# A two-layer RWKV-7 / mLSTM trunk on one core: the triangular inversion on all four quarters of TensorE, and layer norms scaled in one VectorE step

## What is computed

```python
def _layer_norm(x, g, b):
    mu = x.mean(-1); var = mean(square(x - mu))
    return (x - mu) * rsqrt(var + 1e-5) * g + b

def _layer(x, st, w):
    x = _layer_norm(ALPHA * x + 0.5 * _swiglu(x, ffn1...), ln1_g, ln1_b)      # norm 0
    p = x @ w_in
    ya = _rwkv7(p[..., :RWKV_COLS], ...)      # S = S*w + sa (kk*a) + v k per token, 8 heads of 64
    yb = _mlstm(p[..., RWKV_COLS:], ...)      # 4 heads of 128
    x = _layer_norm(ALPHA * x + concat(ya, yb) @ w_out, ln2_g, ln2_b)         # norm 1
    x = _layer_norm(ALPHA * x + 0.5 * _swiglu(x, ffn2...), ln3_g, ln3_b)      # norm 2
```

## Time and profile before

| | us |
|---|---|
| median of 3 runs | 1639.91 (1639.57 to 1642.65) |
| the profiled execution, its own time | 1636.58 |
| its span | 1634.5 |
| PE busy / weight loads busy | 1549.8 (95%) / 1486.7 (91%) |
| DVE / ACT / POOL busy | 865.3 (53%) / 665.4 (41%) / 416.1 (25%) |

### The profile page before, as it was taken

How to read it: one execution, slowest core, us unless ns; L and a number is a source line. 1 busy time by engine, 2 the same in 40 slices (tenths; PEclk the granted TensorE clock), 3 DMA queues, 4 the chain that set the end, 5 groups by cost and what they waited for, 6 DMA issues and landing times.

```text
span 1634.5 us, 34807 instructions
## 1 busy us (share of the span) xinstructions
PE 1549.8 (95%) x13868; PEld 1486.7 (91%) x13868; DVE 865.3 (53%) x1347; ACT 665.4 (41%) x1071; POOL 416.1 (25%) x427
## 2 busy tenths in 40 slices
PE   7999999999998899999899999999999998999994
PEld 7999998998977799999799999989978787999993
DVE  4444436686356764444464444366944577444334
ACT  4333235656432443333343333357563245333323
POOL 6222552013121432221052221020132324222011
PEclk9999999999997899999999999999999899999997
DMA  7455552442122555544354545434330443544420
GB/s 205 144 151 150 160 152 71 124 112 75 28 62 78 149 147 148 154 143 153 103 147 144 151 143 165 118 96 111 96 76 3 115 119 108 164 143 152 148 97 32
DMA packets 307200, 197.75 MB, mean 121 GB/s; under 512 B 7516, under 2 KB 282320, under 8 KB 307096
## 3 DMA queue, kind: packets, MB, share of 16 engines
q1 hardware_dynamic: 303512, 189.64, 39.9%
q0 software_dynamic: 3584, 6.62, 1.6%
HBM read 187.46 MB, written 8.78 MB: 120 GB/s over the span
## 4 chain that ended last, share of the span: by engine, by line
PE 89%; DVE 5%; ACT 3%; POOL 1%; DVEq 1%; issue 1%; DMA 0%; ACTq 0%; POOLq 0%
PE bank L1905 25%; PE bank L1907 24%; PE bank L1906 24%; PE bank L674 1%; PE bank L690 1%; PE bank L585 1%; PE bank L686 1%; PE bank L561 1%; PE bank L1976 1%; POOL xl L2349 1%; PE bank L423 1%; DVE x L2250 1%; PE bank L1978 1%; PE bank L433 1%; DVE z L2248 1%
## 5 line engine op out<-in xcount | busy, mean ns | idle before, releaser
L1905 PE MATMUL bank<-xh,whi 128*128 128x320 f32 x2016 | 632.8, 314 | 31.6 <-POOL xl L2379 24.7
L2217 DVE TENSOR_TENSOR wlo<-raw,whi 128x1024 fp32r<-128x1024 f32 x340 | 428.2, 1262 | 401.2 <-ACT whi L2101 400.5
L1906 PE MATMUL bank<-xl,whi 128*128 128x320 f32 x2016 | 628.5, 312 | 0.0
L1907 PE MATMUL bank<-xh,wlo 128*128 128x320 f32 x2016 | 628.2, 312 | 0.0
L2101 ACT ACTIVATE whi<-raw 128x1024 fp32r<-128x1024 f32 x340 | 359.2, 1060 | 573.9 <-PE bank L1907 569.4
L1905 PEld LDWEIGHTS bank<-xh,whi 128*128 128x128 f32 x2016 | 383.6, 190 | 38.4 <-issue 32.6
L1906 PEld LDWEIGHTS bank<-xl,whi 128*128 128x128 f32 x2016 | 383.8, 190 | 0.5
L1907 PEld LDWEIGHTS bank<-xh,wlo 128*128 128x128 f32 x2016 | 383.4, 190 | 0.0
L2359 POOL TENSOR_TENSOR hl<-scratch,hh 128x320 f32 x88 | 146.1, 1661 | 435.9 <-DVE scratch L2270 435.9
L1905 PE MATMUL bank<-hh,whi 128*128 (+1 forms) x704 | 218.4, 310 | 0.7 <-ACT vec L2137 0.7
L1907 PE MATMUL bank<-hh,wlo 128*128 (+1 forms) x704 | 217.2, 309 | 0.0
(11 more groups left out here) (363 smaller groups left out, 1568.0 us busy)
## 6 DMA issues: line engine op xcount, KB each, us to landing
raw<-in_ffn_wg SPq DMA_DIRECT2D x88, 512.0 KB, 3.8
raw<-in_ffn_wu SPq DMA_DIRECT2D x88, 512.0 KB, 3.8
raw<-in_ffn_wd SPq DMA_DIRECT2D x88, 512.0 KB, 3.6
raw<-in_w_in SPq DMA_DIRECT2D x60, 512.0 KB, 3.8
raw<-in_w_out SPq DMA_DIRECT2D x16, 512.0 KB, 5.4
raw<-in_state_C SPq DMA_DIRECT2D x8, 512.0 KB, 6.5
out_s_C<-raw SPq DMA_DIRECT2D x8, 512.0 KB, 3.5
ring<-in_state_wkv POOLq DMA_DIRECT2D x2, 1024.0 KB, 8.5
```

Source lines behind the costliest of these rows:

```text
L1905: pe.matmul(out, w_hi, hi, start=start, stop=False)
L1906: pe.matmul(out, w_hi, lo, start=False, stop=False)
L1907: return pe.matmul(out, w_lo, hi, start=False, stop=stop)
L2217: dve.tensor_tensor(wlo[:, slot, :], raw[:, slot, :], whi[:, slot, :].bitcast(F32), ALU.subtract).then_inc(lo_ready.sem, 1)
```

## The change

**Norms.** The sums are made with `means` (1/1024 in place of 1), so they are the means. ACT squares the mean from the bank, DVE needs two steps for the variance, copies the mean, and subtracts it from six tiles in pairs ahead of the root. One DVE step (`scalar_tensor_tensor`) multiplies a tile by gain and root; ACT adds the bias into `xh`; DVE makes `xl` = (z + bias) - xh itself (`low`), one tile later; POOL has no part in it. ACT writes the full `x` of all eight tiles after the eight `xh`. `first_chunks` does the two passes with `xh` as soon as `xh` of a k is there, and that with `xl` one k later. The last norm makes only `x`, on ACT, and the turns at the end wait for it.

**Inversion.** `xx` keeps, for half q, xi in rows q and xti in the other rows, so that both are in one area of 128 partitions; `copy_growth` makes two copies of 256 columns, from bank 2 + q each (banks 0 and 1 too in the first level), where one of 512 was made. `grow` issues its 16 matmuls in turns over all four quarters of the array; `product`, `samples_u` and the recurrence's products use the crossed quarters. `grow` of step n now waits for the copy of step n - 1. `first_growth` makes 16 matmuls for xi and xti, where 8 and a DVE mask were. POOL's `memory_term` is cut into two halves of 64 columns.

```diff
         def first_growth(pe, L, c):
             pe.wait_ge(t1_ready.sem, t1_ready.by(L, c + 1))
@@
             for j in range(NJ):
-                for part in PART:
-                    last = pe.matmul(bank[2 + c % 2][part, j * CH:(j + 1) * CH], xti[part, c, j, :],
-                                     ident[part, part], start=True, stop=True)
+                for q, part in enumerate(PART):
+                    pe.matmul(bank[growth_bank(c) + q][part, j * CH:(j + 1) * CH], t1[part, c, j, :], ident[part, part],
+                              start=True, stop=True)
+                for q, part in enumerate(PART):
+                    last = pe.matmul(bank[growth_bank(c) + q][PART[1 - q], j * CH:(j + 1) * CH], ident[part, part],
+                                     t1[part, c, j, :], start=True, stop=True)
@@ def grow(pe, L, n):
-            pe.wait_ge(x_copied.sem, x_copied.by(L, n - 1))
-            if lv < NLV[c] - 1:
-                for j in range(NJ):
-                    for part in PART:
-                        pe.matmul(bank[2 + n % 2][part, j * CH:(j + 1) * CH], xti[part, c, j, :], t1[part, c, j, :],
+            pe.wait_ge(x_copied.sem, x_copied.by(L, n))
+            for j in range(NJ):
+                if lv < NLV[c] - 1:
+                    for q in range(2):
+                        pe.matmul(bank[2 + q][PART[q], j * CH:(j + 1) * CH], xti(q, c, j), t1[PART[1 - q], c, j, :],
                                   start=True, stop=True)
-            for j in range(NJ):
-                for part in PART:
-                    last = pe.matmul(bank[2 + n % 2][part, (NJ + j) * CH:(NJ + j + 1) * CH], t1[part, c, j, :],
-                                     xti[part, c, j, :], start=True, stop=True)
+                for q in range(2):
+                    last = pe.matmul(bank[2 + q][PART[1 - q], j * CH:(j + 1) * CH], t1[PART[1 - q], c, j, :],
+                                     xti(q, c, j), start=True, stop=True)
@@ def copy_growth(act, L, n):
-            lo, hi = int(lv == NLV[c] - 1), 1 + int(lv > 0)
-            act.activation(xx[:, c, lo:hi, :, :].rearrange("p x j s -> p (x j s)"),
-                           bank[2 + n % 2][:, lo * NJ * CH:hi * NJ * CH], ACT.Copy).then_inc(x_copied.sem, 1)
+            for q in range(2):
+                rows = slice(0, P) if lv < NLV[c] - 1 else PART[1 - q]
+                last = act.activation(xx[rows, c, q, :, :].rearrange("p j s -> p (j s)"), 
+                                      bank[growth_bank(n) + q][rows, 0:NJ * CH], ACT.Copy)
+            last.then_inc(x_copied.sem, 1)
@@ def first_chunks(base, which, outs):  (PE)
-                    for k in range(KT):
-                        pe.wait_ge(x_ready.sem, x_ready.by(L, KT * (which - 1) + k + 1))
-                        for n in range(LOOK):
-                            last = three_passes(pe, outs[n], slot_of(L, base + n), k * P, xh[:, k, :], xl[:, k, :],
+                    for k in range(KT + 1):
+                        if k < KT:
+                            pe.wait_ge(xh_ready.sem, xh_ready.by(L, before + k + 1))
+                            for n in range(LOOK):
+                                slot = slot_of(L, base + n)
+                                for w in (whi, wlo):
+                                    pe.matmul(outs[n], w[:, slot, k * P:(k + 1) * P], xh[:, k, :],
+                                              start=(k == 0 and w is whi), stop=False)
+                        if k:
+                            pe.wait_ge(x_ready.sem, x_ready.by(L, before + k))
+                            for n in range(LOOK):
+                                last = pe.matmul(outs[n], whi[:, slot_of(L, base + n), (k - 1) * P:k * P],
+                                                 xl[:, k - 1, :], start=False, stop=(k == KT))
@@ def layer_norm(which):  (ACT)
+                    act.wait_ge(stats_ready.sem, stats_ready.by(L, which + 1))
+                    act.activation(rstd, LN_SUMS[which][0][:, 0:T], ACT.Square).then_inc(msq_ready.sem, 1)
@@
-                        act.activation(xh[:, o, :], z[:, o, :], ACT.Identity, scale=g, bias=b).then_inc(
-                            xh_ready.sem, 1)
+                        if not last_norm:
+                            act.activation(xh[:, o, :], z[:, o, :], ACT.Identity,
+                                           bias=vec[:, g0 + KT + o:g0 + KT + o + 1]).then_inc(xh_ready.sem, 1)
+                    for o in range(KT):
+                        act.activation(x[:, o, :], z[:, o, :], ACT.Identity,
+                                       bias=vec[:, g0 + KT + o:g0 + KT + o + 1]).then_inc(xf_ready.sem, 1)
@@ def layer_norm(which):  (DVE)
+                    dve.wait_ge(msq_ready.sem, msq_ready.by(L, which + 1))
+                    dve.scalar_tensor_tensor(out=var, in0=sums[1], scalar=eps, in1=rstd,
+                                             op0=ALU.add, op1=ALU.subtract)
+                    dve.drain()
+                    dve.tensor_scalar(var, var, eps, None, ALU.max).then_inc(var_ready.sem, 1)
+                    dve.tensor_copy(mean, sums[0])
...
+                    for o in range(0, KT - 2, 2):
+                        dve.tensor_tensor(z[:, o:o + 2, :], z[:, o:o + 2, :],
...
-                        dve.tensor_tensor(z[:, o, :], z[:, o, :], rstd, ALU.mult).then_inc(norm_ready.sem, 1)
-                        if o + 4 < KT:
-                            dve.tensor_tensor(z[:, o + 4, :], z[:, o + 4, :], mean, ALU.subtract)
+                        dve.scalar_tensor_tensor(out=z[:, o, :], in0=z[:, o, :], scalar=vec[:, g0 + o:g0 + o + 1],
+                                                 in1=rstd, op0=ALU.mult, op1=ALU.mult).then_inc(norm_ready.sem, 1)
+                        if o + 6 < KT:
+                            dve.tensor_tensor(z[:, o + 6, :], z[:, o + 6, :], mean, ALU.subtract)
                         dve.drain()
-                        dve.tensor_scalar(x[:, o, :], z[:, o, :], g, b, ALU.mult, ALU.add).then_inc(xf_ready.sem, 1)
+                        if o and not last_norm:
+                            low(o - 1)
```

More of the change, by code:

```diff
@@ L633, in side @@
                     for j in range(NJ):
-                        for q, part in enumerate(PART):
+                        for q in range(2):
                             at = (n * NJ + j) * NA
-                            last = pe.matmul(b[part, at:at + NA], scores[PART[1 - q], c, j, q, 0, :],
+                            last = pe.matmul(b[PART[1 - q], at:at + NA], scores[PART[1 - q], c, j, q, 0, :],
                                              uv[PART[1 - q], c, j, q, :], start=True, stop=True)
@@ L737, in samples_r @@
             for j in range(NJ):
-                for part in PART:
-                    last = pe.matmul(bank[3][part, j * NA:(j + 1) * NA], s0sum[part, j, 0, :], ident[part, part],
-                                     start=True, stop=True)
+                for q, part in enumerate(PART):
+                    last = pe.matmul(bank[3][PART[1 - q], j * NA:(j + 1) * NA], s0sum[part, j, 0, :],
+                                     ident[part, part], start=True, stop=True)
             last.then_inc(samples_mm.sem, 1)
@@ L746, in samples_u @@
             for j in range(NJ):
-                for part in PART:
-                    last = pe.matmul(bank[3][part, j * NA:(j + 1) * NA], xti[part, NPC, j, :], rsb_s[part, j, :],
+                for q, part in enumerate(PART):
+                    last = pe.matmul(bank[3][part, j * NA:(j + 1) * NA], xti(q, NPC, j), rsb_s[PART[1 - q], j, :],
                                      start=True, stop=True)
@@ L785, in recurrence @@
                     for j in range(NJ):
[L786 to L787 removed]
+                        for q, part in enumerate(PART):
+                            last = pe.matmul(bank[0][PART[1 - q], j * NA:(j + 1) * NA], ar[part, j, c, 0, :],
                                              state[part, c % 2, j, :], start=True, stop=True)
@@ L798, in recurrence @@
                 for j in range(NJ):
-                    for part in PART:
-                        last = pe.matmul(bank[1][part, j * NA:(j + 1) * NA], xti[part, c, j, :], rhs[part, j, :],
+                    for q, part in enumerate(PART):
+                        last = pe.matmul(bank[1][part, j * NA:(j + 1) * NA], xti(q, c, j), rhs[PART[1 - q], j, :],
                                          start=True, stop=True)
@@ L1968, in ln_sums_of_group @@
                     for out, src in zip(LN_SUMS[which], (zsum, sqsum)):
-                        pe.matmul(out[:, 0:T], ones[:, :], src, start=True, stop=False)
+                        pe.matmul(out[:, 0:T], means[:, :], src, start=True, stop=False)
                 def ln_sums(which):
```

101 lines of the change are left out of this document (50 added, 51 removed).

## The result

The changed kernel takes 1631.45 us, median of 5 runs (1629.98 to 1634.21), against 1639.62 of the kernel before (5 runs): ratio 0.9947, 95% interval 0.9932 to 0.9961, **8.2 us faster** where 18.2 were forecast. Two repeats beside the kernel before on other chips gave 0.9925 (0.9902 to 0.9948) and 0.9928 (0.9908 to 0.9949). The mean is 1630.0 over all 17 runs of the changed kernel, against 1641.3 over the 78 runs of the kernel before that stood beside the experiments, so some 11.3 us is the best number for the change. Runs of the changed kernel lie between 1622 and 1634 us, and the first profile of the kernel before stood 5 us under the mean of its kernel: one execution does not size an edit of 8 us.

A forecast was written before the change was run, and what follows sets the result against it. PE was taken as the bound, carrying 89% of the chain of waits. Norms 11.2 plus inversion 7.0 made 18.2 us, taken from the median 1639.91 to give 1621.7 us, range 1615 to 1632.

The forecast's parts named there:

- First scaled tile stays at 564.1: Norm 1: DVE, now later than ACT's root, leaves the first scaled tile's start unchanged; nothing won there.
- PE starts 1.5 us earlier: After a norm: PE waits for `xh` alone, starting 1.2 us after the first scaled tile instead of 2.7.
- They are even; I take 1.35 each, 4.1 in all: Norm 1 (twice), norm 2 of first layer: fourth weight tile ready at 578.4, PE there at 578.3; most of 1.5 kept.
- Rival 1: After norms 1 and 2: ACT's x steps delay the fourth weight tile; norms win 5.6, time 1627.3; chance 0.12.
- Norm 0: First norm of each layer: earlier PE start wins 1.5 us in the first layer and 1.1 in the second.
- Last norm 4.5: Before the turns at the end: without `xh` and `xl`, PE starts at 1620.6 instead of 1625.11, 4.5 us won.
- Norms 11.2: Sum of savings at all norms: 1.5 + 1.1 + 4.1 + 4.5 = 11.2 us, lower bound 5.6.
- A growth 0.52 us: Inversion: a full growth's sixteen matmuls on four quarters take 0.52 us instead of 0.92, saving 0.40.
- rivals 2 and 3: Inversion: four quarters bring nothing, ACT's copies end growths, 1631.7, chance 0.10; floor per matmul, growth 0.8, 1628.3, chance 0.14.
- 3.5 us a layer: Inversion: twelve of seventeen full growths save 0.40 each, 4.8, less copy and wait costs; 3.5 us a layer.
- The same matmuls in less time make PE's activity denser, not thinner: Growth stages: argument that the granted clock would not fall with the new inversion; no cost was taken for it.
- rival 4: Growth stages: granted clock falls, kernel slower; 1692 us if one stage runs at half clock, 1643 if a third of both; chance 0.04.

The follow-up runs named there:

- run 126: Not a run's label: part of "low time of a run 126 to 139 us", time at the lower clock, kernel before against the inversion part alone.
- e17: Changed kernel with mean subtracted from four tiles ahead, ACT's x steps behind the silu, and eight constant products in the wait after norms 1 and 2: 1625.83 us (0.9907).
- e16: Changed kernel with mean subtracted from four tiles ahead and ACT's x steps after norms 1 and 2 moved behind the stage's first silu: 1623.65 us (0.9893).
- e9: Changed kernel with fourth tile's split ahead of x, four tiles ahead, and eight constant products in the wait after norms 1 and 2: 1631.04 us (0.9925).

## Why the prediction was wrong

The direction and the two largest mechanisms were right, the size was not: 18.2 us forecast, 8.2 measured in the result, 11.3 over all runs.

- *First scaled tile stays at 564.1*: right, 563.93, with DVE the later one; four tiles ahead brought 0.5 (forecast 0.4).
- *PE starts 1.5 us earlier*: right, 6.80 us after the sums' first product where it was 8.34.
- ***"They are even; I take 1.35 each, 4.1 in all"***: this step failed. PE did keep its early start through three tiles: it was ready at 577.35, where 578.3 was forecast. It then lost it to the fourth tile, ready at 579.0. After norm 1, norm to norm was 244.4 us against 244.8 to 245.0, 0.4 to 0.6 a place; after norm 2 of the first layer it was 249.0 against 248.9 and 249.6. That is about 1.2 us in all and not 4.1. Rival 1 named the place, but for a wrong reason: ACT's x steps took 3.72 us, as forecast; the last `xh` came late, because DVE's scaling, subtraction and low part take 1.04, 1.5 and then 1.10 us a tile, 8.1 us to the eighth and not 7.3. And I looked at the fourth tile only; the second split, the table load and the silu stood behind x too, so the fifth tile was the next bound.
- *Norm 0*: from the sums to the gate product 23.4 us instead of 24.4, about 1.0 won in each layer (forecast 1.5 and 1.1).
- *Last norm 4.5*: right; from the sums to the end 27.0 us (28.0 in one of three profiles) against 32.1, the wait 14.0 instead of the forecast 13.6.
- *Norms 11.2*: measured 7.7.
- *A growth 0.52 us*: right; rivals 2 and 3 are out, and so are copies of ACT that end most steps.
- *3.5 us a layer*: at equal clock 3.3 and 5.6. Layer 0 holds PE's wait of 2.1 us for "issue" inside one early growth; every profile of the new inversion has it there (0.8 to 2.8 us), none of the four of the old one has. It does not explain the clock: in layer 1 the twelve profiles have at most 0.9 us of it, most of them 0.3 or none, and their low time is as high.
- ***"The same matmuls in less time make PE's activity denser, not thinner"***: the second step that failed, the argument against rival 4. The low time of a stage was 16.8 us on average, where it was 6.8 or 10.2 with the old inversion. I had priced the clock only as a disaster of 21 us, so it got 0.04 as "slower" and no place as a cost within the forecast. The size was off as well: at the price named there, one more us for each us of groups, 21.5 us is a sixth of two stages of 70 us and not a third, and the stages are 86 us long. Inversion 7.0 forecast, 3.2 measured, low time of a run 126 to 139 us.
- *The range* of 1615 to 1632 held 1631.45, at its edge. That is partly luck: its upper end stood for rivals 1 to 3 and not for the clock.

## What to carry to other kernels

When a wait is moved off PE, follow the engine that took over the work to everything queued behind it, not just to the first product it delays: here splits, a table load and a silu stood behind eight steps whose result PE did not need there. Price the granted clock as a term with a sign of its own: compare stages by length less half of their time at the lower level, over several profiles, before believing a gain or a loss of a few us. This holds in stages where PE is busy nearly all the time; over a whole run low time also stands in PE's waits, where it costs nothing (e17 has 10 us less of it than e16, at the same time). And test two suspects together as well as singly; here each alone showed half a microsecond at most.

## What the runs showed of the hardware

- Stages of the same code differ by up to 6 us, most of it with the granted clock (layer 0: 85.2 to 91.3 us, and within 2.3 at equal clock). The Trainium skill ("TensorE: Matmul & The Clock Gate", What's actually happening) says that the clock follows how busy PE has been. By the rows PE's busy share in these stages was 0.90 in the changed kernel against 0.93 before, so these rows agree in direction. The kernel with constant products in the growth does not fit so simply: busy 0.94 and 0.95, low time 10.2 and 13.7 us. Which activity counts, no run here shows.
- Sixteen 64x64 f32 matmuls with 64 columns took 0.52 us on four quarters and 0.92 on two; a growth in two passes began 0.71 us ahead of the group behind it.
- With constant products after a norm the first chunks ran at the full clock (0.31 us records instead of 0.47). In e9 the lower clock came back 20 us later in two of three places, after PE had waited 2.2 us; in e17, where that wait is 0.2 us, it did not.
- The "issue" wait in the growth of layer 0 (2.1 us at 417.4) begins as a 1 MB state load leaves the DMA engines (their share is 0.02 during the wait), and within a microsecond of a packet of the instruction queue (416.5 to 417.5). The old kernel has such packets too and no such wait. Its cause was not tried.
